# Index query low parts and causal additions moved into the next block's first units, and a late join of the last small block's sum

## The reference

```python
proj = x @ w_in                      # q, k, v, index query, index key, index weights, conv gates and input
# for each block of 128 queries; 8 index heads of 64
dots  = einsum('bqhd,bsd->bqhs', qi_b, ki) * 64 ** -0.5
score = einsum('bqh,bqhs->bqs', w_b, relu(dots))
score = where(key_pos <= qpos, score, -inf)      # causal
_, idx = top_k(score, 256)
# softmax attention of 8 heads x 64 over the selected keys
logits = where(valid, q_b . k_sel * 64 ** -0.5, -inf); p = softmax(logits); out = p @ v_sel
```

## Time and profile before

| what | value |
|---|---|
| median of 3 runs | 1262.85 us (1262.18 to 1263.8) |
| the profiled execution | 1260.8 us, span 1259.0 us |
| PE busy | 1224.8 us, 97% of the span |
| DVE busy | 958.3 us, 76% |
| POOL busy | 661.8 us, 53% |
| ACT busy | 521.0 us, 41% |
| mean granted TensorE clock | 0.997 |

### The profile page before, as it was taken

One profiled execution on the slowest core, in us unless ns is written; L12 is line 12 of the kernel. 1 busy time (PEld: TensorE's weight loads), 2 busy tenths in 40 slices (PEclk: granted clock), 3 DMA queues, 4 the chain that ended last, 5 costly groups with the idle time before them and its releaser, 6 DMA issues.

```text
span 1259.0 us, 17040 instructions
## 1 busy us (share of the span) xinstructions
PE 1224.8 (97%) x6037; PEld 1030.0 (82%) x6037; DVE 958.3 (76%) x1549; ACT 521.0 (41%) x911; POOL 661.8 (53%) x544
## 2 busy tenths in 40 slices
PE   8989999999998999999999999999999999999997
PEld 7967788888887899788778888888888888888885
DVE  3687999999978889437867776776776766565897
ACT  4375322221339789503533323333323333553351
POOL 2240666698779541108678666666666630020744
PEclk9999999999999999999999999999999999999999
DMA  5231222211002112424135545544445448966664
GB/s 202 72 89 33 51 51 60 67 33 46 24 17 52 35 28 74 160 74 152 51 127 167 175 139 172 175 142 160 161 134 191 159 152 292 358 190 196 198 189 166
DMA packets 121404, 157.66 MB, mean 125 GB/s; under 512 B 7252, under 2 KB 81256, under 8 KB 119912
## 3 DMA queue, kind: packets, MB, share of 16 engines
q1 hardware_dynamic: 121320, 156.57, 38.8%
HBM read 109.09 MB, written 40.11 MB: 119 GB/s over the span
## 4 chain that ended last, share of the span: by engine, by line
PE 89%; DVE 6%; ACT 2%; issue 2%; DMA 1%; POOL 0%; SPq 0%; DVEq 0%; ACTq 0%; POOLq 0%
PE banks L694 26%; PE banks L696 26%; PE banks L695 26%; PE banks L908 2%; PE banks L959 2%; DVE scores L1886 1%; PE banks L859 1%; PE banks L927 1%; PE banks L928 1%; PE banks L876 1%; PE banks L877 1%; PE banks L710 1%; DVE pt L1983 1%; PE banks L1036 0%; DMA xs<-in_x 0%
## 5 line engine op out<-in xcount | busy, mean ns | idle before, releaser
L1902 DVE TENSOR_SCALAR_CACHE_REDUCE mask<-scores,small 128x384 bf16<-128x384 f32 (+1 forms) x186 | 163.7, 943 | 1.1
L2235 DVE TENSOR_TENSOR step_lo<-step_raw,step_hi 128x1024 fp32r<-128x1024 f32 x77 | 110.4, 1454 | 57.0 <-ACT step_hi L1455 56.2
L1689 POOL TENSOR_TENSOR ring_lo<-sum,ring_hi 128x512 fp32r<-128x512 f32 x88 | 122.0, 1389 | 59.8 <-ACT ring_hi L1390 59.7
L694 PE MATMUL banks<-act_hi,ring_hi 128*128 128x512 f32 x352 | 137.0, 389 | 0.0
L696 PE MATMUL banks<-act_hi,ring_lo 128*128 128x512 f32 x352 | 136.9, 389 | 0.0
L695 PE MATMUL banks<-act_lo,ring_hi 128*128 128x512 f32 x352 | 136.9, 389 | 0.0
L1689 POOL TENSOR_TENSOR ring_lo<-gu_raw,ring_hi 128x512 fp32r<-128x512 f32 x66 | 94.4, 1431 | 73.2 <-ACT ring_hi L1390 73.2
L1455 ACT ACTIVATE step_hi<-step_raw 128x1024 fp32r<-128x1024 f32 x77 | 81.7, 1061 | 111.0 <-DMA step_raw<-in_w_down 56.1
L1390 ACT ACTIVATE ring_hi<-sum 128x512 fp32r<-128x512 f32 x88 | 55.1, 630 | 161.7 <-POOL sum L1700 61.8
L694 PE MATMUL banks<-step_hi 128*128 128x512 f32 x308 | 119.9, 389 | 0.0
L696 PE MATMUL banks<-step_hi,step_lo 128*128 128x512 f32 x308 | 119.8, 389 | 0.0
(11 more groups left out here) (268 smaller groups left out, 3159.3 us busy)
## 6 DMA issues: line engine op xcount, KB each, us to landing
gu_raw<-in_w_gate_up SPq DMA_DIRECT2D x44, 512.0 KB, 5.2
step_raw<-h_store SPq DMA_DIRECT2D x77, 256.0 KB, 3.0
wd_raw<-in_w_down SPq DMA_DIRECT2D x11, 1024.0 KB, 5.0
h_store<-hid SPq DMA_DIRECT2D x11, 1024.0 KB, 3.9
step_raw<-wd_store SPq DMA_DIRECT2D x44, 256.0 KB, 3.6
wd_store<-wd_raw SPq DMA_DIRECT2D x11, 768.0 KB, 3.4
h_store<-h_sum SPq DMA_DIRECT2D x11, 768.0 KB, 5.4
step_raw<-in_w_down SPq DMA_DIRECT2D x33, 256.0 KB, 3.1
```

Of the source, the lines that this page charges most:

```text
L694: pe.matmul(dst, a[0], b[0], start=first, stop=False)
L1689: pool.tensor_tensor(ring_lo[:, slot], src, ring_hi[:, slot].bitcast(F32), ALU.subtract).then_inc(ring_low, 1)
L1902: c = dve.tensor_scalar(mask[:, part(b)], scores[:, part(b)], threshold(j), 0.0, ALU.is_ge, ALU.add, accum_out=count[:, j:j + 1])
L2235: dve.tensor_tensor(step_lo[n][:], step_raw[n][:], step_hi[n][:].bitcast(F32), ALU.subtract).then_inc(step_low, 1)
```

## The change

`idx_low(b)` is cut into `query_low(b, odd)` (one 64x512 subtraction) and `key_low(b)`. In the loop of the score stage, the low parts of block b + 2 are no longer made at the end of block b. They are made one block later, inside block b + 1: one query part after its head 0, the other and the key part after its head 1. The causal addition of block b is made after head 3 of block b + 1 (that of block 7 stays at the end). ACT's and PE's instructions are as before, and so are their waits. In the attention stage the copy and the addition that end `sum_last_small(1)`, with their waits, become `join_last_small()`, called one step later (36), behind that step's mask and low parts.

```diff
--- before.py
+++ after.py
@@ -1848,15 +1848,16 @@
                        ).then_inc(idx_rotated, 1)
                 dve.wait_ge(idx_rotated, b - SEL[0] + 1)
 
-            def idx_low(b):
+            def query_low(b, odd):
                 dve.wait_ge(idx_hi, b + 1)
-                q_bank, k_bank = IDX_BANKS.get(b, (4, 5))
+                q_bank, own = IDX_BANKS.get(b, (4, 5))[0], half_of(odd)
                 if q_bank is not None:
-                    for odd in range(2):
-                        own = half_of(odd)
-                        dve.tensor_tensor(qi_lo[own, b % 2, odd::2, :],
-                                          ps[own, q_bank, :].rearrange("p (c s) -> p c s", c=CT),
-                                          qi_hi[own, b % 2, odd::2, :].bitcast(F32), ALU.subtract)
+                    dve.tensor_tensor(qi_lo[own, b % 2, odd::2, :],
+                                      ps[own, q_bank, :].rearrange("p (c s) -> p c s", c=CT),
+                                      qi_hi[own, b % 2, odd::2, :].bitcast(F32), ALU.subtract)
+
+            def key_low(b):
+                k_bank = IDX_BANKS.get(b, (4, 5))[1]
                 lower = ki_hl[HD:P, b * P:(b + 1) * P]
                 dve.tensor_tensor(lower, ps[HD:P, k_bank, 0:P], lower.bitcast(F32), ALU.subtract).then_inc(idx_lo, 1)
 
@@ -1867,6 +1868,19 @@
                     x_lower(b + 4)
             rotate_first_heads(2)
             rotate_first_heads(3)
+            def idx_low(b):
+                query_low(b, 0)
+                query_low(b, 1)
+                key_low(b)
+
+            def add_causal(b):
+                n = (b + 1) * P
+                s = scores[:, OFF[b]:OFF[b] + n]
+                dve.wait_ge(score_added, (b - SEL[0] + 1) * HEADS)
+                if b == SEL[0]:
+                    dve.wait_ge(const_made, 1)
+                link(dve.tensor_tensor(s[:, b * P:n], s[:, b * P:n], causal[:], ALU.add))
+
             for b in range(3):
                 idx_low(b)
             rotate_first_heads(4)
@@ -1885,13 +1899,13 @@
                         dve.wait_ge(score_added, i)
                         dve.scalar_tensor_tensor(s, relu[i % 2][:, 0:n], w, s, ALU.mult, ALU.add
                                                  ).then_inc(score_added, 1)
-                dve.wait_ge(score_added, i + 1)
-                if b == SEL[0]:
-                    dve.wait_ge(const_made, 1)
-                link(dve.tensor_tensor(s[:, b * P:n], s[:, b * P:n], causal[:], ALU.add))
-                if b + 2 < NB:
-                    idx_low(b + 2)
-
+                    if b > SEL[0] and h < 2 and b + 1 < NB:
+                        query_low(b + 1, h)
+                        if h == 1:
+                            key_low(b + 1)
+                    if b > SEL[0] and h == 3:
+                        add_causal(b - 1)
+            add_causal(NB - 1)
 
 
             def part(b):
@@ -2017,13 +2031,19 @@
                 link(dve.reciprocal(rinv[:, heads], rsum[:, first_col:first_col + half]))
                 dve.tensor_tensor(target, low, scale, ALU.mult)
                 dve.tensor_tensor(high, high, scale, ALU.mult).then_inc(halves_scaled, 1)
-                dve.wait_ge(halves_scaled, b + part + 1)
                 if part == 0:
+                    dve.wait_ge(halves_scaled, b + 1)
                     dve.tensor_tensor(target, high, target, ALU.add).then_inc(half_summed, 1)
-                else:
-                    dve.wait_ge(half_summed, 1)
-                    dve.tensor_copy(o_row[:, 0:half, :], half_row[:])
-                    dve.tensor_tensor(target, high, target, ALU.add).then_inc(heads_summed, 1)
+
+            def join_last_small():
+
+                b, half = SMALL - 1, HEADS // 2
+                target = o_row[:, half:HEADS, :]
+                dve.wait_ge(half_summed, 1)
+                dve.tensor_copy(o_row[:, 0:half, :], half_row[:])
+                dve.wait_ge(halves_scaled, b + 2)
+                dve.tensor_tensor(target, OUT_SMALL[b % 2][:, half:HEADS, 0, :], target, ALU.add
+                                  ).then_inc(heads_summed, 1)
 
             def sum_heads(b):
 
@@ -2101,6 +2121,8 @@
                     turned_low(c)
                 if i == LARGE0 + 3:
                     sum_last_small(1)
+                if i == LARGE0 + 4:
+                    join_last_small()
                 if 2 <= TURN_AT.get(i - 1, 0) < 6:
                     copy_q(TURN_AT[i - 1])
                 if i % HEADS == 7 and i >= 15:
```

## The result

The changed kernel takes 1264.8 us (median of 22 runs) against 1262.14 us of the kernel before (22 runs): a ratio of 1.0021, interval 1.0015 to 1.0027, or +2.65 us. Forecast were +4.25 us, 1267.1 us and "slower". The 1264.8 us lie in the stated range (1264.4 to 1268.7) but under the forecast's own (1265.6 to 1268.4): 0.7 us of that is the kernel before, which stands at 1262.14 us with 22 runs where 3 had given 1262.85, and 1.6 us is the change. The ratio is just over the 0.2% from which the forecast called a change slower, and its interval reaches under it. Single runs of one kernel spread over 4 us; the traces show where the time of one execution goes to 0.1 us, and I go by them for the terms of the sum.

The account below looks back on a forecast made before the run. It took DVE to bound the score stage up to about unit 34 and PE after it. 2.2 + 2.4 - 0.35 = +4.25 us on 1262.85 gave 1267.1 us; own range 1265.6 to 1268.4, stated range 1264.4 to 1268.7.

Parts of the forecast that it names:

- The bound: Score stage: DVE paces it up to about unit 34, then PE is late until the stage ends.
- The path to unit 34: Ends of blocks 2 to 4: DVE idles for ACT's relu, making relu 32 later by 2.2 us (1.5 to 3.0).
- The wait at unit 34: PE's first extra matmuls wait for block 7's key low part, now behind two scores: 2.4 us (1.5 to 2.8).
- The join: Attention stage: copy and addition one step later gain 0.35 us (0 to 0.85), as they now delay unit 37's mask.
- first rival: PE's wait at unit 34 isn't felt, only the block ends count: +1.85, 1264.7 us; chance 0.09.
- the wait wouldn't be felt: Unit 34: PE comes late to its wait or the key part comes early; 1264.7 us, chance 0.09.
- nothing moves but the join: Score stage unchanged because ACT gets ahead and fills DVE's idle times; 1262.5 us, chance 0.05.
- the stage gets faster: Score stage: ACT's waits at the starts of blocks 3 to 6 go, and PE's with them; 1257.2 us, chance 0.05.
- The late transfers: Score stage: SP's transfers of low parts land after PE needs them; part of a rival at 1268.5 to 1271 us, chance 0.08.
- The score moved next to POOL: Near 75 us: moved scores blocked by up to three POOL instructions of 0.46 us; part of a rival, chance 0.08.
- the last rival: Score stage slower still, by POOL blocking moved scores or transfers landing late: 1268.5 to 1271 us; chance 0.08.

Follow-up runs that it names:

- e11: e8 with DVE's three low parts one each after heads 1, 2 and 3 and the causal addition after head 4; ratio to the kernel before 1.0013.
- e6: Kernel before with only block 7's low parts moved, to after heads 0 and 1 of block 6; ratio to the kernel before 1.0027.
- e3: Changed kernel with block 7's low parts made at the end of block 5 as before; ratio to the kernel before 0.9997.
- e9: Changed kernel with PE's extra matmuls begun at unit 36, four per unit, not at 34 with three; ratio to the kernel before 1.0003.
- e2: Kernel before with only the join one step later; ratio to the kernel before 0.9999.
- e12: Kernel before with only the later join, a second set of rounds; ratio to the kernel before 0.9998.
- e1: Changed kernel with the join put back where it was, so the score stage part only; ratio to the kernel before 1.0034.
- e10: The changed kernel itself, run again in a second set; ratio to the kernel before 1.0035.
- e8: Changed kernel with ACT's high parts behind the next block's second relu, DVE's low parts behind head 1, block 7's as before; ratio to the kernel before 0.9998.
- e5: Changed kernel with ACT's high parts behind the next block's second relu, DVE's low parts behind head 1, extra matmuls from unit 36; ratio to the kernel before 0.9998.

## Why the prediction was right, and where it was not

**The bound.** That DVE paces the score stage up to unit 34 and PE from there, and that nothing up to the attention stage has slack, held: from the threshold search to the mask of unit 0 it is 245.6 to 245.7 us in all twelve profiles.

**The path to unit 34: forecast 2.2, measured 1.0 us.** The idle times came as worked out, a bit larger (0.59, 0.98, 0.92 for 0.47, 0.88, 0.81). The failed step is the sentence that DVE has "the same instructions in both kernels" up to the score addition of unit 29. The same instructions, but not the same gaps. In block 4, before, the eight scores run from 85.32 to the causal addition at 92.83, 7.51 us:

```profile
85.32 0.55 DVE L1883 TENSOR_SCALAR scores<-relu,small 128x640 f32<-128x640 f32 x1
...
85.98 6.82 DVE L1886 SCALAR_TENSOR_TENSOR scores<-relu,small,scores 128x640 f32<-128x640 f32 x7
```

After, the block runs from 85.22 to 94.22 (95.14 less the 0.92 of idle time), 9.00 us, for the eight scores and 2.06 us of moved work: 0.57 us less than the sum. Of that, 0.1 us is the wait for ACT's high parts at 83.6, which the forecast had taken off. For the rest, the groups by form show the seven additions before (85.4 to 92.7 us) and after (85.4 to 94.2 us), with busy time, mean ns and idle time ahead of them:

```profile
L1886 DVE SCALAR_TENSOR_TENSOR scores<-relu,small,scores 128x640 f32<-128x640 f32 x7 | 6.2, 884 | 0.7
...
L1900 DVE SCALAR_TENSOR_TENSOR scores<-relu,small,scores 128x640 f32<-128x640 f32 x7 | 6.2, 882 | 0.5
```

An addition waits for the one before it, since it reads what that one wrote, and 0.10 us of idle time stand ahead of each in a row of them: 0.99 us from start to start. The prediction counted this gap as 0.05. An instruction that waits for nothing of the one before it starts up to 0.08 us ahead of that one's recorded end (0.07 at 86.41, against 85.80 + 0.68). So from the addition at 86.41 to the query low part at 87.31 it is 0.90 us, and the two from 88.25 to the causal addition at 90.04 take 1.79. The timeline merges over so short a gap, and the groups give it no releaser. The same count gives 0.4 us of saving in block 3 and 0.5 in block 5. So DVE's idle times were 2.5 us, 0.3 more than forecast, and some 1.4 us of them were won back inside the blocks. That saving is read from the rows; the run meant to test it (e11) was spoilt.

The Trainium skill, VectorE: DVE Perf Modes, The DRAIN you can't avoid, says that a semaphore after each of a chain of copies costs nothing over one semaphore after the last. That is another comparison than the one here: each score addition raises its semaphore in both kernels, and what differs is whether the next instruction waits for it. No run here tests the page's sentence. The rows show that an addition with no wait behind it is 0.09 us shorter from start to start (0.90 for 0.99).

**The wait at unit 34: forecast 2.4, measured 2.1 as a wait, and 2.3 as the later start of the first extra matmul** (e6: 41.3 for 39.0). Right, for the reason given; e3 and e9 each take it away in another way.

**Not in the forecast: the fall of the clock, 1.6 us.** From the first extra matmul to the threshold search it is 28.6 to 28.7 us in the four kernels with the wait and 27.0 to 27.1 in before, e2, e3 and e12. The forecast looked at how long PE would stand, not at what it would run at afterwards.

**The join: forecast 0.35, measured 0.95 us in the traces.** The mis-sized step is the mask of unit 37. I charged the join with the 0.85 us it took before. After, copy and addition take 0.53 us from start to start (440.64 to 441.17), and the low parts 0.80. The copy itself is 0.28 us, where it was 0.60. In all twelve profiles it is 0.59 or 0.60 us where POOL's addition started 0.02 us ahead of it (before, e1, e6), and 0.28 or 0.29 us in the nine others, where nothing of POOL's ran beside it. Before:

```profile
433.38 0.47 POOL L1626 TENSOR_TENSOR ot_sum<-ot 128x128 f32<-128x128 f32 x1 [5.62 <-ACT ot L1305]
```

and after:

```profile
439.21 0.46 POOL L1626 TENSOR_TENSOR ot_sum<-ot 128x128 f32<-128x128 f32 x1 [5.62 <-ACT ot L1305]
```

POOL's began 0.02 us before DVE's copy (433.40) in the kernel before, and was over 0.97 us before it (440.64) after. The Trainium skill, SBUF — State Buffer, Who interferes with whom, says that a DVE copy can use the port pair that it shares with GpSimd, and that whoever starts first blocks the other for its whole instruction: by that the copy waited for POOL, and the trace agrees: it ended at 434.00, 0.15 us after POOL's addition. With the join short, the mask of unit 37 was early enough for PE to keep its step of 2.07 us, and no part of the gain was lost there. The gain itself was 0.98 us at the mask of unit 36, not 0.85: it starts 0.33 us behind the start of the last scaling, where it was 1.31, since the copy had waited for that scaling too.

**Sum.** Forecast 2.2 + 2.4 - 0.35 = 4.25; the traces have 1.0 + 2.3 + 1.6 - 0.95 = 3.95. The sum was good because a term that was too large by 1.2 and a gain that was too small by 0.6 stood against a cost that was missing, of 1.6. That is luck: the first term and the join lie outside their own bounds (1.5 to 3.0, and 0 to 0.85), and the clock isn't in the sum. The 22 runs say 2.65 us, the five of e10 4.4 (2.9 to 6.1). Why the larger set is 1.3 us under the traces isn't settled; the clock of its single stretches wasn't recorded. The time alone wouldn't have told the forecast from its first rival, which has 1264.7 us. The lower end of the forecast's own range, 1265.6, doesn't follow from its terms either: 3.3 - 0.85 gives 1265.3.

**Rivals.** That the wait wouldn't be felt, that nothing moves but the join, and that the stage gets faster are all out by e3, e6 and the trace. The late transfers were not seen in the changed kernel, but e9, with the same order on DVE, has one of 0.4 us, and e11 shows what they cost. The score moved next to POOL wasn't blocked: the one at 76.94 took 0.73 us, and the mean of the seven of that size before, by the groups by form, was 0.755. But the moved causal addition of block 2 was held beside POOL's rotation, and so was the first of the scores behind it:

```profile
80.18 0.54 DVE L1882 TENSOR_TENSOR scores<-scores,causal 128x128 f32<-128x128 f32 x1
...
80.76 3.48 DVE L1900 SCALAR_TENSOR_TENSOR scores<-relu,small,scores 128x512 f32<-128x512 f32 x4
```

The causal addition took 0.42 us in its old place, also beside POOL, and 0.28 in e11, where POOL didn't run beside it; the first of the four scores took 0.90, 0.14 over the mean. So the mechanism of the last rival is there, at some 0.3 us over the old places (0.12 and 0.14), and is part of the 1.0 us.

## What to carry to other kernels

Time that an engine spends on its own work while its next input is being made isn't a stall, and moving the work away only bares the wait; look first at what the other engine does in that time. (Moving that, in e8 and e5, did take the idle time away, and was worth no time that could be measured.) When work is put off, list every wait on the semaphore that it raises, above all one that is just due now: here a weight load's 0.2 us was the sign of a wait of 2.1. And price a pause of PE at more than its length, since the clock may be lower for a while behind it.

## What the runs showed of the hardware

A pause of 2.1 us in PE's work, after some 40 us in which PE had been busy 85% of the time (32.96 of the 39 us from 66 to 105 in the profile after), was followed by the lower clock for part of the next 10 us, four times out of four. Pauses of at most 1.3 us in the same stage, 5.3 to 6.1 us of them in sum, as before and in e3 and e9, never were.

There is a second such place, at 620 to 640 us, where PE pauses for 3 to 5 of 20 us in every kernel, and there it varies from one profile to the next: the granted clock of that stretch was 1.00 in e1, 0.95 in e10, 0.91 before, 0.89 after and 0.83 in e9. The stretch from the first ring part to the last (574 to 1024 us before) took 447.7 us in e1 and 449.2 to 450.6 in the others. That is as large as the effects studied here, in a place whose instructions none of the kernels changes. It is a likely part of the 4 us over which single runs of one kernel spread, though no timed run has the clock by stretch: of the 26 runs of the kernel before beside e6, the four with a mean clock of 0.998 took 1259.5 to 1260.3 us and the ten with 0.996 took 1262.0 to 1263.9.
